# Memory attention of the samples: value products on four column groups, and value tiles in places of their own

## The reference, cut to what matters

```python
def _cross_attn(x, mk, mv, wq, wo):
    q = (x @ wq).reshape(b, l, MEM_HEADS, MEM_HD)
    s = jnp.einsum('bqhd,bkhd->bhqk', q, mk).astype(jnp.float32) * (MEM_HD ** -0.5)
    p = jax.nn.softmax(s, axis=-1).astype(mv.dtype)
    o = jnp.einsum('bhqk,bkhd->bqhd', p, mv).reshape(b, l, MEM_HEADS * MEM_HD)
    return o @ wo
...
        yp = _post(yp, _cross_attn(yp, mk, mv, w_xq[i], w_xo[i]), ln_x_g[i], ln_x_b[i])
        ys = _post(ys, _cross_attn(ys, cache_mem_k[i], cache_mem_v[i], w_xq[i], w_xo[i]), ln_x_g[i], ln_x_b[i])
```

## Time and profile before

| | us |
|---|---|
| median of 3 runs | 3855.66 |
| lowest, highest | 3851.53, 3861.66 |
| the profiled execution | 3853.86 |
| its span in the trace | 3852.1 |
| granted TensorE clock, mean | 0.945 of full speed |

### The profile page before, as it was taken

One profiled execution on the slowest core, in us unless ns is written; L12 is line 12 of the kernel. 1 busy time (PEld: TensorE's weight loads), 2 busy tenths in 40 slices (PEclk: granted clock), 3 DMA queues, 4 the chain that ended last, 5 costly groups with the idle time before them and its releaser, 6 DMA issues.

```text
span 3852.1 us, 54394 instructions
## 1 busy us (share of the span) xinstructions
PE 3407.9 (88%) x21246; PEld 3188.3 (83%) x21246; DVE 1465.0 (38%) x2169; ACT 1002.0 (26%) x1311; POOL 398.6 (10%) x283
## 2 busy tenths in 40 slices
PE   7985789799989999999699966797999799999996
PEld 6973458796889999999689955696978799999996
DVE  1555444524342222223403457856144522122226
ACT  2123442423131011011313323435132311111112
POOL 1664102000200000001000033010001000000001
PEclk9987999999989999999899989899999899999997
DMA  4673641324111111111121114322261111111111
GB/s 133 205 239 120 229 146 46 115 97 165 45 31 46 44 48 45 44 44 38 47 77 60 55 52 148 126 66 85 68 225 38 33 44 44 49 44 44 44 38 56
DMA packets 366737, 319.80 MB, mean 83 GB/s; under 512 B 19681, under 2 KB 308882, under 8 KB 366212
## 3 DMA queue, kind: packets, MB, share of 16 engines
q1 hardware_dynamic: 346527, 295.66, 24.8%
q10 hardware_dynamic: 19940, 21.96, 1.7%
q0 software_dynamic: 144, 0.52, 0.0%
HBM read 287.69 MB, written 30.74 MB: 83 GB/s over the span
## 4 chain that ended last, share of the span: by engine, by line
PE 76%; DVE 10%; DMA 4%; issue 4%; ACT 3%; POOL 1%; SPq 1%; DVEq 0%; ACTq 0%; POOLq 0%
PE ps L319 63%; PE ps L1652 2%; PE ps L1674 1%; DVE spl_w L304 1%; PE ps L977 1%; DVE x L1447 1%; PE ps L705 1%; PE ps L1027 1%; DMA raw_w<-in_w_xv 1%; PE ps L1047 1%; PE ps L1630 1%; DVE acc L2273 1%; ACT x L1461 1%; POOL kpage L1100 1%; DVE prob L992 1%
## 5 line engine op out<-in xcount | busy, mean ns | idle before, releaser
L319 PE MATMUL ps<-xs,spl_w 128*128 128x344 f32 x12456 | 1992.4, 322 | 44.3 <-DVE spl_w L304 25.8
L319 PEld LDWEIGHTS ps<-xs,spl_w 128*128 128x128 f32 x12456 | 1986.3, 190 | 47.2 <-DVE spl_w L304 27.8
L304 DVE TENSOR_TENSOR spl_w<-raw_w,spl_w 128x1024 fp32r<-128x1024 f32 x268 | 337.6, 1260 | 759.3 <-ACT spl_w L300 754.8
L319 PE MATMUL ps<-hs,spl_w 128*128 128x344 f32 x3168 | 514.5, 325 | 27.5 <-DVE hs L1866 27.5
L319 PEld LDWEIGHTS ps<-hs,spl_w 128*128 128x128 f32 x3168 | 513.0, 193 | 29.1 <-issue 29.1
L300 ACT CAST spl_w<-raw_w 128x1024 fp32r<-128x1024 f32 x268 | 279.3, 1042 | 392.1 <-PE ps L319 360.4
L1864 DVE TENSOR_TENSOR sum_x<-sq,ps 128x1032 f32<-128x1032 f32 x44 | 54.1, 1229 | 351.4 <-PE ps L319 351.4
L1401 POOL MEMSET sum_x<- 128x1032 f32 x6 | 5.9, 982 | 1648.9 <-DVE hs L1866 1452.5
L1848 ACT CAST hs<-sum_x 128x1032 f32 (+1 forms) x44 | 46.4, 1056 | 472.1 <-DVE sum_x L1864 472.1
L1409 POOL TENSOR_TENSOR sum_x<-sum_x,x 128x1032 f32<-128x1032 f32 x48 | 116.1, 2418 | 479.8 <-DVE x L1369 187.5
L1100 POOL TENSOR_TENSOR kpage<-kpage,qb 128x1024 f32<-128x1024 f32 x64 | 155.1, 2447 | 94.4 <-DMA kpage<-in_cache_fox_k 94.3
(11 more groups left out here) (362 smaller groups left out, 2925.6 us busy)
## 6 DMA issues: line engine op xcount, KB each, us to landing
kpage<-in_cache_fox_k SPq DMA_DIRECT2D x128, 256.0 KB, 3.4
vpage<-in_cache_fox_v SPq DMA_DIRECT2D x128, 256.0 KB, 2.9
raw_w<-in_w_gate SPq DMA_DIRECT2D x44, 512.0 KB, 3.8
raw_w<-in_w_up SPq DMA_DIRECT2D x44, 512.0 KB, 3.8
mkv<-in_cache_mem_k SPq DMA_DIRECT2D x16, 1024.0 KB, 7.7
mkv<-in_cache_mem_v SPq DMA_DIRECT2D x16, 1024.0 KB, 5.1
raw_w<-in_w_down SPq DMA_DIRECT2D x32, 512.0 KB, 4.0
raw_w<-in_w_in_cd SPq DMA_DIRECT2D x28, 512.0 KB, 3.8
```

Source lines behind the costliest of these rows:

```text
L304: dve.tensor_tensor(spl_w[:, s, 1], raw_w[:, s], spl_w[:, s, 0].bitcast(F32), ALU.subtract).then_inc(lo_ready, 1)
L319: mm = pe.matmul(ps[:, 3 * s + t, 0:width], spl_w[:, s, a, k], part[:, k, width * t:width * (t + 1)], start=(k == 0 and step == 0), stop=( ...
```

## The change

The value products are no longer made sample by sample: for each half of the samples, each half of the keys and each half of the columns, four products follow each other, of four samples, into partitions 0 to 31, 32 to 63, 64 to 95 and 96 to 127. DVE's mask then works on all 128 partitions with the small `sel_h` (made once at the start) in place of `own_x`, and `sel_b` sums over all 128. `mv_used` counts 2 in each layer instead of 9.

All eight value tiles have places: 0 to 3 in `mkv` as before, 4 in `qbx`, 5 and 6 over `mem_s` (`v_by_mem`), 7 over `sum_x` and `sum_sq` (`v_by_sums`). SP issues tiles 5, 6 and 7 behind the query rows of samples 4, 5 and 6, and tile 4 behind the last key. POOL's clears of `sum_x` and `sum_sq` wait for the products.

DVE makes the keys of samples 3 and 4 in unit 3 and then one sample a unit, so that unit 7 has none; the maximum over the samples stands in unit 7, and the subtraction ahead of the last multiplication.

The diff without the list of step names and without part of its context:

```diff
--- before.py
+++ after.py
@@ -108,7 +108,8 @@
         smx = sb("smx", [P, DECB, 2, MH])
-        sel_b = sb("sel_b", [MH * DECB, DECB])
+        sel_b = sb("sel_b", [P, DECB])
+        sel_h = sb("sel_h", [P, MH])
         sel_row = sb("sel_row", [P, 4])
@@ -140,6 +141,9 @@
         rest = ExitStack()
+        v_by_sums = sb("v_by_sums", [P, 2, D], F32, rest)
+        rest.close()
+        rest = ExitStack()
         sum_x = sb("sum_x", [P, TOK], F32, rest)
@@ -152,6 +156,9 @@
         qx = sb("qx", [P, DC, TOK], F32, ln_rest)
+        under_mem = ExitStack()
+        v_by_mem = sb("v_by_mem", [P, 2, 2, D], F32, under_mem)
+        under_mem.close()
         mem_s = sb("mem_s", [P, 2, DC, NMEM], F32R, ln_rest)
@@ -183,7 +190,6 @@
         qn_area.close()
-        own_x = sb("own_x", [MH * DECB, MH, MD], F32, xs_area)
         smz = sb("smz", [P, DECB, 2, MH, DECB], F32, xs_area)
@@ -470,9 +476,10 @@
             dve.reciprocal(inv_cnt[:], inv_cnt[:]).then_inc(dve_steps, mark("inv_cnt_ready"))
-            n = MH * DECB
-            dve.tensor_reduce(sel_b[:], ident[0:n, 0:n].rearrange("p (h b) -> p b h", h=MH), AX.X, ALU.add
+            dve.tensor_reduce(sel_b[:], ident[:].rearrange("p (g b) -> p b g", b=DECB), AX.X, ALU.add
                               ).then_inc(dve_steps, mark("sel_b_ready"))
+            dve.tensor_reduce(sel_h[:], ident[:].rearrange("p (q h b) -> p h q b", h=MH, b=DECB), AX.XY, ALU.add
+                              ).then_inc(dve_steps, mark("sel_h_ready"))
             dve.tensor_reduce(sel_row[:], ident[:].rearrange("p (j m h) -> p m j h", j=4, h=FH), AX.XY, ALU.add
@@ -1397,6 +1404,8 @@
                 pool.wait_ge(sem("xs_lo"), XS_LO_MIXER[ln // 3])
+            if ln in (1, 4):
+                pool.wait_ge(sem("mv_used"), 2 * (ln // 3) + 1)
             then = chain(pool, "pool")
@@ -1599,20 +1608,34 @@
             sp.wait_ge(tile_done, 2 * G1[f"xq{L}"])
-            for f in range(2 * DECB):
+            def values(b, s):
+                sp.dma_start(v_tile(b), A["cache_mem_v"][L, b].rearrange("(a p) h d -> p a (h d)", p=P)).then_inc(s, 16)
+
+            for f in range(DECB):
                 if f >= 4:
-                    if f - 4 < DECB:
-                        sp.wait_ge(sem("mk_used"), DECB * L + f - 3)
-                    else:
-                        sp.wait_ge(sem("mv_used"), (DECB + 1) * L + f - 3 - DECB)
-                cache = A["cache_mem_k"] if f < DECB else A["cache_mem_v"]
-                sp.dma_start(mkv[:, f % 4], cache[L, f % DECB].rearrange("(a p) h d -> p a (h d)", p=P)).then_inc(sem(f"mkv_loaded{f % 4}"), 16)
-                if f < DECB:
-                    if f == 0:
-                        sp.wait_ge(sem("q_stored"), 16 * (L + 3))
-                    if f >= 2:
-                        sp.wait_ge(sem("mk_used"), DECB * L + f - 1)
-                    sp.dma_start(qbx[:, f % 2], qx_d[L][f:f + 1, :].to_broadcast([P, D])).then_inc(sem(f"q_row_loaded{f % 2}"), 16)
+                    sp.wait_ge(sem("mk_used"), DECB * L + f - 3)
+                sp.dma_start(mkv[:, f % 4], A["cache_mem_k"][L, f].rearrange("(a p) h d -> p a (h d)", p=P)).then_inc(sem(f"mkv_loaded{f % 4}"), 16)
+                if f == 0:
+                    sp.wait_ge(sem("q_stored"), 16 * (L + 3))
+                if f >= 2:
+                    sp.wait_ge(sem("mk_used"), DECB * L + f - 1)
+                sp.dma_start(qbx[:, f % 2], qx_d[L][f:f + 1, :].to_broadcast([P, D])).then_inc(sem(f"q_row_loaded{f % 2}"), 16)
+                if 4 <= f <= 6:
+                    values(f + 1, sem("x_back"))
+            for b in range(4):
+                sp.wait_ge(sem("mk_used"), DECB * L + b + 5)
+                values(b, sem(f"mkv_loaded{b}"))
+            sp.wait_ge(sem("mk_used"), DECB * (L + 1))
+            values(4, sem("x_back"))
+
+        def v_tile(b):
+            if b < 4:
+                return mkv[:, b]
+            if b == 4:
+                return qbx[:]
+            if b < 7:
+                return v_by_mem[:, b - 5]
+            return v_by_sums[:]
 
@@ -1667,17 +1690,23 @@
             pe.wait_ge(sem("x_exp"), MH * (N0 + NT))
-            for b in range(DECB):
-                pe.wait_ge(sem(f"mkv_loaded{b % 4}"), 16 * (4 * L + 2 + b // 4 + 1))
+            for half in range(2):
+                if half:
+                    pe.wait_ge(sem("x_back"), 32 + 64 * (L + 1))
+                else:
+                    for b in range(4):
+                        pe.wait_ge(sem(f"mkv_loaded{b}"), 16 * 3 * (L + 1))
                 for a in range(2):
                     for r in range(2):
-                        mm = pe.matmul(ps[0:MH * DECB, r, :], smz[:, b, a].rearrange("p h b -> p (h b)"),
-                                       mkv[:, b % 4, a, 512 * r:512 * (r + 1)], start=(b == 0 and a == 0),
-                                       stop=(b == DECB - 1 and a == 1))
-                mm.then_inc(sem("mv_used"), 1)
+                        for q in range(4):
+                            b = 4 * half + q
+                            mm = pe.matmul(ps[MH * DECB * q:MH * DECB * (q + 1), r, :], smz[:, b, a].rearrange("p h b -> p (h b)"),
+                                           v_tile(b)[:, a, 512 * r:512 * (r + 1)], start=(half == 0 and a == 0),
+                                           stop=(half == 1 and a == 1))
+            mm.then_inc(sem("mv_used"), 1)
             pe.wait_ge(sem("smx_dve_step"), 5 * L + 5)
             for c in range(DC):
-                mm = pe.matmul(ps[:, 2, DECB * c:DECB * (c + 1)], probx[0:MH * DECB, 0, P * c:P * (c + 1)], sel_b[:],
+                mm = pe.matmul(ps[:, 2, DECB * c:DECB * (c + 1)], probx[:, 0, P * c:P * (c + 1)], sel_b[:],
                                start=True, stop=True)
@@ -1710,7 +1739,7 @@
                     act.activation(smx[:], smx[:], ACT.Exp).then_inc(sem("smx_exp"), 1)
-            act.wait_ge(sem("mv_used"), (DECB + 1) * (L + 1))
+            act.wait_ge(sem("mv_used"), 2 * (L + 1))
             act.copy(qx[:, :, SEQ:TOK], ps[:, 2, 0:64].rearrange("p (c b) -> p c b", c=DC)).then_inc(sem("x_out"), 1)
@@ -1721,7 +1750,7 @@
             def keys(b):
-                dve.wait_ge(sem(f"mkv_loaded{b % 4}"), 16 * (4 * L + b // 4 + 1))
+                dve.wait_ge(sem(f"mkv_loaded{b % 4}"), 16 * (3 * L + b // 4 + 1))
                 dve.wait_ge(sem(f"q_row_loaded{b % 2}"), 16 * (DECB // 2 * (L + 1) + b // 2 + 1))
@@ -1730,7 +1759,12 @@
 
+            flat = "p b a h -> p b h a"
             for i in range(NT + 1):
+                if i == NT:
+                    dve.wait_ge(sem("smx_pool_step"), 3 * L + 2)
+                    dve.tensor_tensor(smx[:], smx[:], smr[:, 1].unsqueeze(2).to_broadcast([P, DECB, 2, MH]),
+                                      ALU.subtract).then_inc(sem("smx_dve_step"), 1)
                 if i < NT:
@@ -1745,16 +1779,15 @@
                                       ALU.mult).then_inc(sem("x_prob"), 1)
-                if i < NT:
-                    keys(i)
-
-            dve.wait_ge(sem("mk_used"), DECB * (L + 1))
-            flat = "p b a h -> p b h a"
-            then(dve.tensor_reduce(smr[:, 0], smx[:].rearrange(flat), AX.X, ALU.max))
-            dve.sem_inc(sem("smx_dve_step"), 1)
-            dve.wait_ge(sem("smx_pool_step"), 3 * L + 2)
-            dve.tensor_tensor(smx[:], smx[:], smr[:, 1].unsqueeze(2).to_broadcast([P, DECB, 2, MH]),
-                              ALU.subtract).then_inc(sem("smx_dve_step"), 1)
+                if i < NT - 1:
+                    keys(i if i < 4 else i + 1)
+                    if i == 3:
+                        keys(4)
+                if i == NT - 1:
+                    dve.wait_ge(sem("mk_used"), DECB * (L + 1))
+                    then(dve.tensor_reduce(smr[:, 0], smx[:].rearrange(flat), AX.X, ALU.max))
+                    dve.sem_inc(sem("smx_dve_step"), 1)
+
             dve.wait_ge(sem("smx_exp"), L + 1)
@@ -1763,23 +1796,18 @@
             ins.then_inc(sem("smx_dve_step"), 1)
-            dve.wait_ge(sem("mv_used"), (DECB + 1) * L + DECB)
+            dve.wait_ge(sem("mv_used"), 2 * L + 1)
+            dve.wait_ge(dve_steps, step("sel_h_ready"))
             dve.wait_ge(sem("x_turned"), NT * (L + 1))
-            dve.tensor_tensor(probx[0:MH * DECB, 0].rearrange("p (h d) -> p h d", h=MH),
-                              ps[0:MH * DECB, 0:2, :].rearrange("p a (h d) -> p (a h) d", d=MD),
-                              own_x[:], ALU.mult).then_inc(sem("smx_dve_step"), 1)
+            dve.tensor_tensor(probx[:, 0].rearrange("p (h d) -> p h d", h=MH),
+                              ps[:, 0:2, :].rearrange("p a (h d) -> p (a h) d", d=MD),
+                              sel_h[:].unsqueeze(2).to_broadcast([P, MH, MD]), ALU.mult).then_inc(sem("smx_dve_step"), 1)
             for k in range(DC):
...
         def pool_cross(pool, L):
-            then = chain(pool, "pool")
             pool.wait_ge(sem("q_stored"), 16 * (L + 3))
```

(9 more changed lines are left out.)

## The result

| | before | after |
|---|---|---|
| median, us (4 runs each, taken together) | 3853.60 | 3815.74 |
| lowest, highest | 3850.65, 3861.66 | 3812.16, 3825.20 |
| profiled execution, its span | 3853.86, 3852.1 | 3812.16, 3810.3 |

The ratio is 0.9899, with a 95% interval of 0.9879 to 0.992: 38 us less, 1.0%. The span fell by 41.8 us. The chain in order of time (start, us, what) shows where; the four lines from 917.54 to 930.59 answer to the earlier trace rows, the products of layer 1 (2846.04) to the earlier trace rows.

The account below looks back on a forecast made before the run. TensorE bounds the kernel, its value products unhidden. Per layer -27.65 + 7.05 + 1.0 = -19.6 us, twice -39.2, from 3853.86 (profiled) and 3855.66 (median) gives 3814.7 and 3816.5; predicted 3815, range 3808 to 3827.

Parts of the forecast that it names:

- The products: Memory attention's value products, four in four partition groups: 27.65 us a layer become 7.05, as 8 sets in a row.
- The bound of lone sets: Upper bound for the tiled value products: 8 sets that each pay start and end, 8 x 1.10 = 8.8 us.
- rivals 1, 2 and 5: Value products: sets don't chain, 3819 us (0.10); clock at 1.2 GHz, 3828 us (0.05); still one by one, 3856-3858 us (0.04).
- The lateness of the keys: Key 7 lands at 898.2 at 330 GB/s, so TensorE's turn behind unit 7 loses 1.0 us a layer (0 to 2.2).
- rival 3: Keys or values arrive later than worked out; at 260 GB/s TensorE loses 7.8 us a layer, 3828 us; chance 0.09.
- The keys on DVE: Unit 3 takes two keys at 2.85 us each, hidden; units 4 to 6 stay some 2 us ahead of TensorE.
- the tight place: Unit 7, behind key 7: its multiplication ends at 903.6, while TensorE wants it at 902.32, with 0.3 us free.
- Rival 4: Values ahead of the last three keys make TensorE wait; at 150 GB/s 31 us lost a layer, 3876 us; chance 0.03.
- What was costed at nothing: Masking on 128 partitions (1.22 us), 16 small products (1.96 us), 6.0 us gap before projection and value arrival: no cost.

## Why the prediction was right

The forecast was 3814.7 us for the profiled run and 3816.5 for the median; they were 3812.16 and 3815.74. The runs of the changed kernel lie 13 us apart, so that the median came within 1 us is luck; the terms below are what can be held against the forecast. By its steps:

- The products: 7.05 us from a chain of two sets in another line; measured 7.05 in both layers, at a grant of 1.00. The bound of lone sets (8.8) did not hold, and rivals 1, 2 and 5 fall with it. The untiled run (27.60 us) shows that the tiling, not the places, makes it so. The factor of 3.07 that the Trainium skill gives ("TensorE: Matmul & The Clock Gate", section "Measured speedup vs the span model") was passed by this chain: 27.60 / 7.05 is 3.9.
- The lateness of the keys, 1.0 us a layer: this term was mis-sized, and it makes 2.0 of the 2.5 us by which the profiled run was missed. Measured 0. The failed step is the rate: I took 330 GB/s from stretches that moved 293 and 237. The data of key 7 were there at 894.66, not 898.2; 8.4 MB from 872.8 on are 385 GB/s, and the stretch of 880 to 890 shows 408. So the maximum of unit 7 started at 898.13 instead of near 901, the turn at 902.37 instead of 903.5, and rival 3, a lower rate, did not come. What bounds the rate wasn't tried. The Trainium skill ("DMA: Bandwidth & Descriptors", section "Where 436 GB/s comes from") gives 435 GB/s for the ports into SBUF and has about 358, on the side of HBM, bind such loads; the 408 here, query rows counted in, lies between the two.
- The keys on DVE: that unit 3 hides a second key is right (the run without it is equal). That unit 7 is the tight place fits the rows, by little: 2.3 us to spare behind key 7 (0.61 + 1.67) against 2.9 behind key 5. No run delayed key 7 alone; transfers that stand ahead of all three keys made TensorE wait for key 5.
- Rival 4, values ahead of keys: its mechanism and its price of about one for one were shown by adding transfers, and it lacked a term, the 1.9 and 2.5 us that TensorE lost behind its wait to a lower clock. Its point was 23 us away (key 7 at 894.66 against 917.8).
- What was costed at nothing: the masking on 128 partitions took 1.23 us with a clear of POOL beside it (924.73), the 16 small products 1.97, the first projection product followed the end of the products by 6.0 us, and the values were there in time: right in each.

## What to carry to other kernels

A tiled product already in the kernel, read as a chain and not as a single set, gives the price of the new one. Whoever puts transfers ahead of others should look at each consumer's slack one by one; the first behind the new bytes decides, and a wait on TensorE can cost its length and some slow microseconds more. Go round all four groups of columns, with no more than four passes of one in a row. Two by two, with never more than two passes of a group in a row, still cost 8.84 us, since the other two groups start only when these have four passes left.

## What the runs showed of the hardware

Products on different groups of 32 columns go side by side even if they aren't neighbours in the program: one group with four unfinished passes is what holds up those behind, as 15.79, 8.84, 7.05 and 7.10 us for four orders show.

POOL's first addition behind a reduction over partitions starts 6.6 to 7.2 us late whatever its size, while clears in between don't: 6.98 us for 128x1032; 6.94 and 6.60 in the two layers of one run, 7.14 and 6.91 in those of another, for 128x4. The Trainium skill ("GPSIMD Engine Reference", section "2.1 Instruction dispatch") tells of about 6 us at the first call of a freshly loaded routine; the size is near, and no run here shows that this is the cause.

The same two stretches of 10 us moved 353 and 408 GB/s, at shares of 0.97 and 1.02 of the DMA engines, with tiles of values in the queue, and 293 and 237, at shares of 0.93 and 0.71, without.

TensorE's granted clock fell from 1.00 to 0.50 (2.4 to 1.2 GHz) in or behind waits of 2.55, 12.85 and 16.22 us; of two waits of 2.4 us ahead of the second projection tile one was followed by 0.50 (958.98 to 962.40 in the changed kernel) and one was not (the run with one sample after the other).
